# Mixture-of-experts stage of a hybrid encoder layer: the eight larger experts sorted over all groups, and five rooms of 64 rows instead of four

## What is computed

```
glogits = h2 @ w_group + b_group          # 4 groups, the best one is taken
elogits = h2 @ w_expert + b_expert        # 4 experts in the group, the best two are taken
expert  = g_idx * 4 + top_i               # 16 experts, 1024 * 2 = 2048 pairs of token and expert
hid     = silu(xb @ w_gate[e]) * (xb @ w_up[e])     # 1024 -> 512
out     = (hid @ w_down[e]) * weight                # 512 -> 1024
y       = x + sum of the two experts' out per token
```

## Time and profile before

| | |
|---|---|
| median of 3 runs | 1260.51 us (1259.11 to 1264.08) |
| profiled execution, its own time | 1264.07 us |
| its span in the profile | 1262.4 us |
| TensorE busy | 1178.4 us, 93% of the span |
| stage of the experts | from about 815 us to the end |
| first gate product | 827.18 us |
| plain place, period | 21.9 us |
| place with a room, period | 33.95 us |

### The profile page before, as it was taken

The page is one execution under the profiler, slowest core; times in us unless marked ns, Lnnn a source line. Parts: engine busy times, 40 slices in busy tenths (PEclk is TensorE's granted clock), DMA queues, the critical chain, the costliest instruction groups (busy, mean ns, idle before and its releaser), DMA issues. The chain is left out here.

```text
span 1262.4 us, 24205 instructions
## 1 busy us (share of the span) xinstructions
PE 1178.4 (93%) x9814; PEld 661.4 (52%) x9814; DVE 556.6 (44%) x1332; ACT 308.2 (24%) x791; POOL 200.3 (16%) x234
## 2 busy tenths in 40 slices
PE   5999999999998898899999999489999999999986
PEld 5534444444443666799984555334444444445543
DVE  4358446899694555455773245511222111111111
ACT  5153115422311666533431122100000000000000
POOL 0201310300000324100000011220110424322111
PEclk9989999999998899999999999689999999999989
DMA  9311522142202723234424811469998999863543
GB/s 321 100 38 47 175 60 70 57 143 97 54 34 85 170 70 107 59 104 114 118 75 163 355 68 68 167 231 422 363 372 347 354 369 340 311 269 112 199 143 110
DMA packets 107593, 216.51 MB, mean 172 GB/s; under 512 B 37194, under 2 KB 72474, under 8 KB 103128
## 3 DMA queue, kind: packets, MB, share of 16 engines
q1 hardware_dynamic: 82344, 133.54, 30.1%
q0 software_dynamic: 16688, 47.84, 11.2%
q10 hardware_dynamic: 8448, 33.56, 7.9%
HBM read 186.09 MB, written 36.10 MB: 176 GB/s over the span
## 5 line engine op out<-in xcount | busy, mean ns | idle before, releaser
L520 PE MATMUL pj_ps<-hT,pj_w 128*128 128x512 f32 x576 | 253.6, 596 | 0.0
L520 PEld LDWEIGHTS pj_ps<-hT,pj_w 128*128 128x128 f32 x576 | 108.1, 191 | 135.7 <-issue 135.1
L2135 PE MATMUL ex_py<-wd,ex_hT 128*128 128x512 f32 x256 | 114.4, 600 | 0.0
L1402 PE MATMUL ps_out<-w_out,mixT 128*128 128x512 f32 x256 | 112.3, 594 | 2.1 <-PEq L2489 1.8
L2370 DVE TENSOR_TENSOR ex_hid<-ex_pu,ex_sg 128x512 f32<-128x512 f32 x16 | 11.1, 692 | 201.1 <-PE ex_pu L2182 201.1
L2262 ACT ACTIVATE ex_sg<-ex_pg 128x512 f32<-128x512 f32 x16 | 9.6, 597 | 296.7 <-PE ex_pg L2170 296.7
L2170 PE MATMUL ex_pg<-proj 128*128 128x512 f32 x176 | 79.1, 603 | 1.3 <-DVE proj L2309 1.3
L730 DVE RECIPROCAL mixT<-mixT 128x1024 f32<-128x1024 f32 (+1 forms) x11 | 68.9, 6262 | 24.0 <-ACT mixT L650 19.0
L1402 PEld LDWEIGHTS ps_out<-w_out,mixT 128*128 128x128 f32 x256 | 47.9, 190 | 59.5 <-issue 59.4
L2182 PE MATMUL ex_pu<-proj 128*128 128x512 f32 x176 | 77.3, 592 | 0.0
L2135 PEld LDWEIGHTS ex_py<-wd,ex_hT 128*128 128x128 f32 x256 | 48.2, 194 | 54.7 <-issue 54.7
(11 more groups left out here) (349 smaller groups left out, 1970.3 us busy)
## 6 DMA issues: line engine op xcount, KB each, us to landing
wd<-in_moe_w_down ACTq DMA_DIRECT2D x16, 2048.0 KB, 10.1
proj<-in_moe_w_gate SPq DMA_DIRECT2D x11, 2048.0 KB, 10.4
proj<-in_moe_w_up SPq DMA_DIRECT2D x11, 2048.0 KB, 10.2
mixT<-in_moe_w_gate SPq DMA_DIRECT2D x6, 2048.0 KB, 10.6
mixT<-in_moe_w_up SPq DMA_DIRECT2D x6, 2048.0 KB
pj_w<-in_w_in SPq DMA_DIRECT2D x18, 512.0 KB, 4.0
proj<-in_x SPq DMA_DIRECT2D x16, 512.0 KB, 10.6
products<-pj_unit POOLq DMA_DIRECT2D x4, 2048.0 KB, 9.8
```

The source lines that it names most:

```text
L520: mm = pe.matmul(ps[:, t % 2, half, :], w_tile(t)[:, n, :], s.hT[:, n, half * 512:(half + 1) * 512], start=(n == 0), stop=(n == KD - 1))
L1402: mm = pe.matmul(s.ps_out[:, t % 2, half * 512:(half + 1) * 512], s.mixT[:, k, t * P:(t + 1) * P], s.w_out[:, k, half * 512:(half + 1) * 5 ...
L2135: mm = pe.matmul(py[:, half, :], hT[:, j, :], wd[e % 2][:, j, half * 512:(half + 1) * 512], start=(j == 0), stop=(j == KF - 1))
```

## The change

1. The eight larger experts (the two larger of each group) are sorted by count over all groups and stand in places 8 to 15 in that order. The first eight places stay as they were.
2. There are five rooms of 64 rows, at places 11 to 15 (`ROOM_ROWS`). The code also has a form for rooms of 32 rows, which these numbers do not use.
3. Since neighbours can now share tokens, `read_rows(e)` for e above 8 is issued only when the writes of place e - 1 and of its room have landed; at place 8, when those of places 4 to 7 have landed. It moved from the head of iteration e - 1 to its end, behind `write_rows(e - 1)`.
4. A room's down product follows its own place's down product at once, into a PSUM bank of its own (`ex_pyr`), and no longer waits for the next place's up product. The turn of the room's hidden rows stands between the two halves of the place's down product.
5. SyncE loads the table entries of two places only; GpSimd loads those of the other twelve in its iteration 0, those of the rooms in iteration 2, and those of the blocks in iterations 3 to 6 (before: 6 to 13). VectorE computes the block tables ahead of place 0 and in iteration 0 (before: iterations 2 and 3).
6. The gather for the first block is issued in iteration 15 ahead of the other two.

```
-ROOMS = NG
+ROOM_ROWS = (64, 64, 64, 64, 64)
+ROOMS = len(ROOM_ROWS)
 FIRST_ROOM = NE - ROOMS
+SORTED = NE // 2
...
+            def written(e):
+                pool.wait_ge(s.row_written[e % NG], 16 * (e // NG + 1))
+                if e >= FIRST_ROOM:
+                    q = e - FIRST_ROOM
+                    pool.wait_ge(s.row_written_o[q % 2], 16 * (q // 2 + 1))
+
             def read_rows(e):
-                if e >= NG:
-                    pool.wait_ge(s.row_written[e % NG], 16 * (e // NG))
+                if NG <= e < SORTED:
+                    written(e - NG)
+                elif e == SORTED:
+                    for before in range(SORTED - NG, SORTED):
+                        written(before)
+                elif e > SORTED:
+                    written(e - 1)
...
             for e in range(NE):
-                if e + 1 < NE:
+                if e + 1 < SORTED:
                     read_rows(e + 1)
+                if e == 0:
+                    for p in range(len(STATIC) + NEXT, NE):
+                        load_entries(p)
...
                 if e == FIRST_ROOM - 1:
                     pool.wait_ge(zeroed, 2)
-                    pool.wait_ge(room_in, 32 * ROOMS)
+                    pool.wait_ge(room_in, 16 * sum(P // n for n in ROOM_ROWS))
                     for q in range(2):
                         room_rows(q)
...
                 write_rows(e)
                 if e >= FIRST_ROOM:
                     write_room(e - FIRST_ROOM)
+                if SORTED <= e + 1 < NE:
+                    read_rows(e + 1)
+                    if e == FIRST_ROOM - 1:
+                        pool.wait_ge(quartered, 1)
+                    if e + 1 >= FIRST_ROOM:
+                        read_room(e + 1 - FIRST_ROOM)
...
-                if behind_room:
-                    down_room(e - 1 - FIRST_ROOM)
-                elif e:
-                    down(e - 1)
+                if e and not behind_room:
+                    for half in range(2):
+                        down(e - 1, half)
...
-                    down(e)
-
-            turn_h_room(ROOMS - 1)
-            n = overflow_count(pe)
-            down_room(ROOMS - 1)
+                        n = overflow_count(pe)
+                    down(e, 0)
+                    turn_h_room(q)
+                    down(e, 1)
+                    down_room(q)
+            pe.wait_ge(summed, NE)
```

More of the change, by code:

```diff
@@ L1538, in out_projection_router @@
         slotf = sb("slotf", [P, 2, 2])
[L1539 to L1542, removed]
+        room = s.proj[:, C_ALL - 1, 512:1024]
+        key, low, high, top = (room[:, n * NE:(n + 1) * NE] for n in range(4))
+        t64 = room[:, 64:128].rearrange("p (a b c) -> p a b c", a=NG, b=NE // NG)
+        orderf = room[:, 128:176].rearrange("p (a e) -> p a e", a=3)
+        t256 = room[:, 256:512].rearrange("p (a b) -> p a b", a=NE)
         unused = sb("unused", [P, 16, ENTRY], I32)
@@ L1738, in order_experts @@
                 dve.tensor_copy(s.order[:, :, :], orderf[:, :, :]).then_inc(s.ordered, 1)
+                for p in range(FIRST_ROOM, NE):
+                    more = ROOM_ROWS[p - FIRST_ROOM] - (ROOM_ROWS[p - FIRST_ROOM - 1] if p > FIRST_ROOM else 0)
+                    if more:
+                        link(dve.tensor_scalar(key[:, :], low[:, :], float(p), float(more), ALU.is_ge, ALU.mult))
+                        if p == FIRST_ROOM:
+                            link(dve.tensor_copy(s.held[:, :], key[:, :]))
+                        else:
+                            link(dve.tensor_tensor(s.held[:, :], s.held[:, :], key[:, :], ALU.add))
             link(dve.memset(unused[:, :, :], 0))
@@ L2053, in _ @@
                 if e == NE - 1:
-                    pool.wait_ge(idx_in, 32 * NOV)
-                    for b in range(3):
+                    for b in range(1, 3):
                         take(b, b, b + 1)
@@ L2065, in _ @@
             for u in range(2):
-                pool.wait_ge(s.row_written_o[u], 16 * ROOMS // 2)
+                pool.wait_ge(s.row_written_o[u], 16 * len(range(u, ROOMS, 2)))
             def rest(b, i, third, turn):
-                u = turn % 2
+                u = (turn + ROOMS) % 2
                 pool.indirect_dma_start(out=acc_o[:, u, :], out_offset=None, in_=halves,
@@ L2212, in block_of_rows @@
                 fixed = len(range(g, NE, GU_SETS))
+                then = (turn + ROOMS + 1) % 2
                 pe.wait_ge(xo_copied, b + (ROOMS + 1))
@@ L2268, in _ @@
                     q = e - FIRST_ROOM
+                    n = ROOM_ROWS[q] * 4
                     act.wait_ge(gated, room_done(q))
@@ L2391, in _ @@
                     finish(e)
-                if e == 2:
-                    overflow_blocks()
-                if e == 3:
+                    finish_room(q)
+                if e == 0:
                     overflow_rows()
-            finish_room(ROOMS - 1)
+                if e == 5:
+                    dve.wait_ge(room_in, 16 * sum(P // n for n in ROOM_ROWS))
+                    dve.tensor_scalar(quarter[:, :, :], idx_r[:, :, HALF_WRITE:HALF_WRITE + 1], 2.0, s.odd, ALU.mult, ALU.add).then_inc(quartered, 1)
             def block_of_rows(b, i, third, turn):
-                u = turn % 2
+                u, v = turn % 2, (turn + ROOMS) % 2
                 dve.wait_ge(silu_o, b + (ROOMS + 1))
```

196 lines of the change are left out of this document (121 added, 75 removed).

## The result

| | before | changed |
|---|---|---|
| median (20 runs each, same chips) | 1260.70 us (1254.47 to 1266.14) | 1265.67 us (1259.58 to 1269.82) |
| profiled execution, its own time | 1264.07 us | 1264.77 us |
| its span | 1262.4 us | 1263.0 us |

The ratio is 1.0041, with a 95% interval of 1.0025 to 1.0057: the changed kernel is slower by 5.2 us (3.1 to 7.2). The forecast was 1.8 us faster. The time lies inside the range of the prediction (1252.5 to 1266.5), but the sign is wrong.

What follows compares the result with a forecast made beforehand. TensorE's own work was taken to set the pace up to place 15. 12.0 + 3.2 + 3.9 + 0.7 - 21.6 = -1.8 us against the median of 1260.51 gave 1258.7 us, range 1252.5 to 1266.5.

Steps and rivals of the forecast that it cites:

- (d): Read waiting for the write of the place before: loop of 17 to 18 us, below 21.9, so costed at nothing.
- The fifth room: All work of one more room falls ahead of the end of the last room's up product: +12.0 us.
- the gap behind the turn: Places 12 to 15: TensorE waits 0.8 us for VectorE's copy of a room's rows, four times: +3.2 us.
- The first room's gather: Place 11: gather behind place 9's write landing; stall 3.2 us replaces 1.3, plus 2.0 for lower clock: +3.9 us.
- Rival 2: Chain of write and read becomes the bound, place 9's write 7.8 us late: 1269.3 us, chance 0.14.
- rival 1: Place 9's write lands after 3.4 us, first room's gather in time, no stall or clock loss: 1253.5 us, chance 0.17.
- The load of the block count: On TensorE ahead of the last down product, with nothing to hide it: +0.7 us, bounds 0 and 1.05.
- The tail: From the last room's up product to the end: 21.4 us instead of 43.0, so -21.6 us.
- (a): Sorting on VectorE takes net 3.2 us longer, hidden under SyncE's wait for the scattered table: nothing, allowed 0 to 1.
- third sign: Prediction is wrong if VectorE's sort holds up the stage's start, with the first gate product later than 827.2 us.
- (b): SyncE issues 2 instead of 14 table loads, GpSimd's 12 lie in iteration 0 while TensorE multiplies: no gain.
- (c): Block tables on VectorE, some 20 steps, sit in its wait for the next up product: costed at nothing.

Runs made afterwards that it cites:

- the second profile: The changed kernel run again without an edit, beside the kernel before: 1268.53 us against 1262.49, ratio 1.0034 (1.0015 to 1.0053).
- the longer sort: Seven more 256-wide steps, result unused, in the sort of the kernel before: 1254.87 us in one execution, against a median of 1252.60 for the kernel before.

## Why the prediction was wrong

**What bounds the kernel.** Right: TensorE's own products up to the last places, and the waits for gathers at a place's end. Plain places kept their 21.9 us, so the read behind the write of the place before (d) was hidden in the first profile. The reads issued behind a landed write took 4.3 to 6.1 us, but one, at place 12, took 10.4, which the prediction had named as a sign of being wrong: VectorE waited 7.1 us for it, TensorE did not.

**The fifth room, +12.0, and the gap behind the turn, +3.2.** Both as forecast: four waits with 3.1 us in total. But the period of a place with a room grew by 1.2 us and not by the 0.8 of the gap. The other 0.4, four times +1.6, was not in the sum. The prediction took the products' durations of the old order for the new one; with the room's down product ahead of the gate product and the down product split into halves, several starts come 0.1 us later. That this order is the cause is argued from the timelines; no run takes it away alone.

**The first room's gather, +3.9: the step that failed.** The mechanism was right and the size was not: 5.4 - 1.3 + 2.0 = +6.1 in the first profile, and 7.8 - 1.3 + 2.3 = +8.8 in the second. The clock's 2.0 was right, and the write's landing too (8.0 against 7.8). Two values were off. The gather's own landing was taken from the earlier trace rows, 4.4 us, the shortest of three figures of which the longest is 5.2; it took 6.0 us, and now it stands right behind a read and another gather of 128 rows instead of behind small table reads (that this is why it took longer is not shown). The other 0.6 us of the first profile lie mostly between the write's landing and the next issue, 0.8 us where the sum had 0.3. And the write of place 9 was taken as punctual; in the second profile it was 3.2 us late. Rival 2 had this chain, with the worst values only, so that its small version was in no number.

The early gathers, a change of one line that takes away this term alone, show that it decided the sign. Without stall and clock the prediction's sum is -7.0 us (its rival 1); measured without them are -5.9 us (-8.6 to -3.2, ratio 0.9953). So the other terms together were right within the interval. The prediction gave stall and clock 3.2 + 2.0 = 5.2 us; they took 7.4 and 10.1 us in the two profiles, and 10.5 us between the medians.

The first rival, a landing under 4.6 us, did not happen; the write took 8.0 us. The Trainium skill (DMA: Bandwidth & Descriptors, section Anatomy of one DMA), by which that rival would have held, gives an estimate of 3.2 us for these 0.5 MB; the trace of the changed kernel has 3.7 us for its fastest write and 8.3 for the median, so it does not agree here either.

**The load of the block count, +0.7.** No wait was seen: 0. The timeline of the last place (above) has no hole ahead of the down product. The sum had no row for this term, only its bounds.

**The tail, -21.6.** Right in size, 22.1 us left instead of 21.4. But the sum did not say what the credit was for. Of it, 12.1 us are the block's work, some 1 us the wait for VectorE's sum ahead of the room's down product, and 7.8 us the wait for the block's gather with its clock. Those 7.8 need no fifth room: four rooms in the new order lose the wait as well, and the kernel before gains 6.5 us (4.0 to 9.1) by an early gather alone. Against the 12.1 stands a room's 13.2. The prediction's "the block's gather is now issued well before it is wanted" names the mechanism, and passed over that it can be had separately.

**Costed at nothing.** (a) holds by the longer sort; some 0.4 us at the stage's start remain unexplained. The first gate product, the prediction's third sign, came 16.4 us after the first step of the sort instead of 15.6. (b) and (c) show no wait. The prediction's own bounds (clock, load, landing, sorting) add up to 1254.2 to 1262.9 and not 1255 to 1262.5, which changes nothing.

Counted up from -1.8: +2.2 for the gather, +1.6 for the restarts, -0.7 for the load, +0.7 for the tail, +0.8 for the start, and +1.4 for the clock at the first product, which is chance, give +4.2 against the +4.3 read. So the forecast's own mechanism held and its sign did not: it balanced some 20 us of cost against 21.6 us of gain, and 2 to 5 us too little for the stall at one gather decided. That the time still fell into the range is no merit of the sum; the range had been drawn wide for the rivals.

## What to carry to other kernels

When one queue in order serves both transfers that wait for a landing and gathers that wait for nothing, put the second kind ahead of the first: here one line was worth 10 us of 1260. When a change with several parts promises a gain, price each part by itself; here, with rooms of 64 rows, the earlier gather of the block was the whole gain within what was measured, and the room that came with it cost as much as the block that it replaced. And size the work to the rows: halving a room to 32 rows took 5.3 us off its place.

## What the runs showed of the hardware

- In seven profiles a wait of TensorE of 4.6 to 7.8 us in the last places was followed each time by a turn of 1.61 to 1.97 us instead of 1.04 to 1.09, and a down product of 8.14 to 8.93 instead of 7.03 us. The granted clock of the stretch from 6 to 8 us behind the start of that turn was 1.00 in each. Waits of 0.8 us, and those of 1.1 to 1.75 us ahead of the first room in the kernel before, left the next product's duration as it was.
- The write of 128 rows of 4 KB landed after 3.7 to 9.8 us in one and the same execution (median 8.3), and one landed after 11.9 us in another.
- Products of a room of 64 rows took 3.67 us (32 instructions of 64 by 256), of a room of 32 rows 1.95 us (64 instructions of 32 by 128): with the room's rows halved, the time was halved too.
- A gate product of 128 rows was followed by the next start after 6.97 us where it came right behind a down product of 64 rows, and after 6.87 us where it came behind one of 128 rows, with no wait in the trace.
